# Eight more prompt tokens by gathered expert rows, and gathers released by TensorE's column blocks

## The reference

```python
def block(hb):
    q = rms_norm(jnp.einsum('td,dq->tq', hb, w_query).reshape(PEER_BLOCK, PEER_HEADS, PEER_DKEY), qnorm_g)
    s1 = jnp.einsum('thc,hnc->thn', q[..., :half], subkeys[:, 0])
    s2 = jnp.einsum('thc,hnc->thn', q[..., half:], subkeys[:, 1])
    v1, i1 = lax.top_k(s1, PEER_TOPK)
    v2, i2 = lax.top_k(s2, PEER_TOPK)
    ...
    sc, ci = lax.top_k(cand, PEER_TOPK)
    e = i1[ci // 16] * PEER_NKEYS + i2[ci % 16]
    g = jax.nn.softmax(sc, axis=-1)
    a = jax.nn.gelu(jnp.einsum('td,ted->te', hb, u[e]), approximate=False)
    return jnp.einsum('te,ted->td', g * a, v[e])
```

## Time and profile before

| | |
|---|---|
| Median of three runs | 1819.66 us |
| The profiled execution | 1820.75 us, span 1818.9 us |
| TensorE busy | 1766.4 us, 97% of the span |
| VectorE / ScalarE / GpSimd busy | 1214.8 / 565.8 / 487.9 us |
| DMA | 394.47 MB, 217 GB/s over the span |
| The costliest line | L2111, matmuls of the v stage |

### The profile page before, as it was taken

One profiled execution on the slowest core, in us unless ns is written; L12 is line 12 of the kernel. 1 busy time (PEld: TensorE's weight loads), 2 busy tenths in 40 slices (PEclk: granted clock), 3 DMA queues, 4 the chain that ended last, 5 costly groups with the idle time before them and its releaser, 6 DMA issues.

```text
span 1818.9 us, 30885 instructions
## 1 busy us (share of the span) xinstructions
PE 1766.4 (97%) x12693; PEld 1305.6 (72%) x12693; DVE 1214.8 (67%) x2531; ACT 565.8 (31%) x944; POOL 487.9 (27%) x531
## 2 busy tenths in 40 slices
PE   8999898999999999999999999999979999999999
PEld 7744446788888888898888888888636666666665
DVE  7559777768989948787365555544336666666664
ACT  1003234502233233545254444443212222222220
POOL 0000201011656710000000000000457676776750
PEclk9999999999999999999999999999979999999999
DMA  4423723012113334666988888775678888888881
GB/s 168 114 85 122 241 94 140 1 73 93 47 70 141 140 141 164 255 255 244 325 293 295 294 298 293 263 262 175 249 272 331 334 335 335 342 334 335 337 335 48
DMA packets 135885, 394.47 MB, mean 217 GB/s; under 512 B 12992, under 2 KB 85936, under 8 KB 123968
## 3 DMA queue, kind: packets, MB, share of 16 engines
q1 hardware_dynamic: 109392, 315.29, 46.9%
q0 software_dynamic: 26352, 77.20, 12.1%
HBM read 316.52 MB, written 75.92 MB: 216 GB/s over the span
## 4 chain that ended last, share of the span: by engine, by line
PE 81%; DVE 13%; DMA 2%; issue 2%; SPq 1%; ACT 1%; DVEq 0%; ACTq 0%
PE psum L2063 32%; PE psum L2111 28%; PE psum L1764 16%; PE psum L2084 2%; DVE u_lo L1517 1%; DMA qrow<-d_q 1%; DMA u_raw<-in_uT 1%; PE psum L1893 1%; DVE kprod L1182 0%; DVE sSc L1183 0%; DVE rest L1444 0%; DVE sdm L1321 0%; PE psum L1916 0%; PE psum L1816 0%; DMA xT<-in_xT 0%
## 5 line engine op out<-in xcount | busy, mean ns | idle before, releaser
L2111 PE MATMUL psum<-w_hl,v_hi 128*128 128x384 bf16 x2048 | 504.2, 328 | 7.9 <-issue 7.9
L2063 PE MATMUL psum<-h_hi,u_hi 128*128 128x260 bf16 x2048 | 394.0, 273 | 4.7 <-DVE u_lo L1517 3.8
L2063 PE MATMUL psum<-h_lo,u_hi 128*128 128x260 bf16 x2048 | 393.8, 273 | 0.0
L2063 PE MATMUL psum<-h_hi,u_lo 128*128 128x260 bf16 x2048 | 393.7, 273 | 0.0
L753 POOL DMA_INDIRECT trow<-in_v,t_lists x136 | 170.7, 1255 | 696.1 <-ACT act_f L971 589.9
L2111 PE MATMUL psum<-w_hl,v_lo 128*128 128x384 bf16 x1024 | 335.8, 328 | 7.0 <-issue 7.0
L2111 PEld LDWEIGHTS psum<-w_hl,v_hi 128*128 128x128 bf16 x2048 | 200.8, 98 | 147.8 <-issue 18.3
L1674 DVE TENSOR_TENSOR v_lo<-v_raw,v_hi 128x1024 bf16<-128x1024 f32 x128 | 148.2, 1219 | 166.0 <-ACT v_hi L988 102.4
L988 ACT ACTIVATE v_hi<-v_raw 128x1024 bf16<-128x1024 f32 x128 | 124.7, 1044 | 373.8 <-PE psum L2111 361.2
L1517 DVE TENSOR_TENSOR u_lo<-u_raw,u_hi 128x1024 bf16<-128x1024 f32 x128 | 154.0, 1217 | 118.1 <-ACT u_hi L959 118.0
L2063 PEld LDWEIGHTS psum<-h_hi,u_hi 128*128 128x128 bf16 x2048 | 196.7, 97 | 35.7 <-DVE u_lo L1517 4.3
(11 more groups left out here) (382 smaller groups left out, 1784.0 us busy)
## 6 DMA issues: line engine op xcount, KB each, us to landing
u_raw<-in_uT SPq DMA_DIRECT2D x32, 2048.0 KB, 9.3
v_raw<-in_v SPq DMA_DIRECT2D x32, 2048.0 KB
wr<-in_w SPq DMA_DIRECT2D x13, 2048.0 KB, 7.5
d_gate<-stage SPq DMA_DIRECT2D x12, 2048.0 KB, 7.2
w_hl<-d_w SPq DMA_DIRECT2D x32, 768.0 KB
g_up<-d_gate SPq DMA_DIRECT2D x18, 768.0 KB, 9.2
d_w<-w_up SPq DMA_DIRECT2D x18, 768.0 KB, 10.3
d_act<-act_f SPq DMA_DIRECT2D x14, 768.0 KB, 4.1
```

The source lines that it names most:

```text
L2063: mm = pe.matmul(upair[n % 2][:, f, 0:HALF], w[g % 2][:, k, c * P:(c + 1) * P], hs[:, k, halves[f]], start=(k == 0 and x == 0), stop=(k == ...
L2111: mm = pe.matmul(ybank[m][:, 0:DENSE], w[g % 2][:, c, m * P:(m + 1) * P], w_hl[g % WRING][:, z, c, :], start=(g == 0 and c == 0 and x == 0 ...
```

## The change

Eight more prompt tokens (384 - 8 = 376 dense, `EXTRA` = 8) go by gathered rows. Their 8 x 128 experts fill eight more slots, 144 in all. They lie on the partitions as (half, head, token), so `x_acc` is folded by a small product with `xsel` in the last group. Twelve more list steps make their lists in `x_lists`, and GpSimd moves these to `t_lists` by 16 small DMAs. Stores and the gates keep 384 columns (`GATED`); only the last matmul operand is cut to 376. There is one pair of gate blocks fewer (47).

The order of the gathers changes too. `w_used` now counts column blocks, eight a group. GpSimd first waits for all stores and the last weighing, sends `LEAD` = 6 gathers of activations, and then one row and one gather of activations in turn, each row after `paced(s)` column blocks. The batch is four slots with four semaphores instead of eight with two. At the start x comes in four loads instead of eight.

```diff
+GATED = SEQ - P
+EXTRA = 8
+DENSE = GATED - EXTRA
+NBLK = GATED // TB
...
+XSLOTS = SSLOTS + EXTRA * H * TOPK // P
+TSLOTS = XSLOTS + H * TOPK
+BATCH = 4
+LEAD = 6
+DOTS = 4
+KEPT = EXTRA + P + DB
+HALVES = P // (EXTRA * H)
...
+def paced(s):
+
+    return max(0, KT * (NG - 2) * s // TSLOTS - 3)
...
-            for k in range(KT):
-                sp.dma_start(xT[:, k, :], I["xT"][:, k, :]).then_inc(x_in[k], 16)
-                if k == 1:
+            for k in range(0, KT, 2):
+                sp.dma_start(xT[:, k:k + 2, :], I["xT"][:, k:k + 2, :]).then_inc(x_in[k // 2], 16)
+                if k == 0:
...
                 if j >= WRING:
-                    sp.wait_ge(w_used, j - WRING + 1)
+                    sp.wait_ge(w_used, KT * (j - WRING + 1))
...
+            for half in range(HALVES):
+                for h in range(H):
+                    at = EXTRA * (H * half + h)
+                    pool.dma_start(t_lists[at:at + EXTRA, :, SSLOTS:XSLOTS],
+                                   x_lists[P - EXTRA:P, :, h * TOPK + half * (XSLOTS - SSLOTS):][:, :, 0:XSLOTS - SSLOTS]
+                                   ).then_inc(s_moved, 16)
...
-            pool.wait_ge(s_moved, 32)
+            pool.wait_ge(s_moved, MOVED)
             pool.wait_ge(a_gelu, NKEYS)
-            for s in range(4):
-                slot_row(s)
             for b in range(2):
                 pool.wait_ge(as_stored[b], 16 * (NG // 2))
                 pool.wait_ge(a_stored[b], 16 * (EARLY // 2))
-            for s in range(BATCH):
+            pool.wait_ge(w_prod, LATE_KEYS)
+            for s in range(LEAD):
                 slot_dot(s)
-            pool.wait_ge(w_prod, LATE_KEYS)
-            for s in range(4, TROWS):
+            for s in range(TSLOTS):
+                if paced(s) > 0:
+                    pool.wait_ge(w_used, paced(s))
                 slot_row(s)
-            for s in range(BATCH, 2 * BATCH):
-                slot_dot(s)
-            for s in range(TROWS, TSLOTS):
-                slot_row(s)
-                if s + 2 * BATCH - TROWS < TSLOTS:
-                    slot_dot(s + 2 * BATCH - TROWS)
+                if s + LEAD < TSLOTS:
+                    slot_dot(s + LEAD)
...
+            tail = slice(P - COLT, P)
+            first, second = idx[tail, NPT - 2, 0, :], idx[tail, NPT - 2, 1, :]
+            sdo(v.tensor_copy(x_gate[tail, :], gt[tail, NPT - 2, :]))
+            sdo(ts(t_who[tail, :], t_who[tail, :], -float(P), None, ALU.add))
+            sdo(ts(t_tmp[tail, 0, :], second, float(KEPT), t_who[tail, :], ALU.mult, ALU.add))
...
+            sdo(v.tensor_reduce(xsel[:, :], ident.rearrange("p (h t) -> p t h", t=EXTRA), AX.X, ALU.add))
...
+                if i == 1:
+                    v.wait_ge(s_moved, MOVED)
...
-                            mm = pe.matmul(ybank[m][:, 0:DENSE], w[g % 2][:, c, m * P:(m + 1) * P], w_hl[g % WRING][:, z, c, :],
+                            mm = pe.matmul(ybank[m][:, 0:DENSE], w[g % 2][:, c, m * P:(m + 1) * P], w_hl[g % WRING][:, z, c, 0:DENSE],
...
                     if g == NG - 1:
                         pe.wait_ge(t_added, TSLOTS)
-                        turn(ybank[m][:, DENSE:SEQ], t_acc[:, m * P:(m + 1) * P], P).then_inc(y_made, 1)
-                    elif m == (3 if g == 0 else KT - 1):
+                        product(ybank[m][:, DENSE:GATED], [(x_acc[:, m * P:(m + 1) * P], xsel[:, :])])
+                        turn(ybank[m][:, GATED:SEQ], t_acc[:, m * P:(m + 1) * P], P).then_inc(y_made, 1)
+                    else:
                         mm.then_inc(w_used, 1)
```

More of the change, by code:

```diff
@@ L200, in trunk_and_peer @@
     t_who = put("t_who", [P, 1], F32, c0 + 4928 + 20 * TSLOTS)
+    xsel = put("xsel", [P, EXTRA], F32, c0 + 8064)
     ones_row = put("ones_row", [H, SEQ], F32, c0)
@@ L356, in trunk_and_peer @@
     t_acc = put("t_acc", [P, D], F32, B0 + 12288)
+    x_acc = put("x_acc", [P, D], F32, B0)
+    x_lists = put("x_lists", [P, 3, P], F32, T0 + 40960)
+    x_vrow, x_arow, x_gate = x_lists[:, 0, :].bitcast(U32), x_lists[:, 1, :].bitcast(U32), x_lists[:, 2, :]
+    assert T0 + 40960 + 1536 <= W0
     upair = [pa[:, 2 * b:2 * b + 2, :] for b in range(2)]
@@ L378, in sems @@
         return [sem(n) for n in names.split()]
-    x_in = [sem(f"x_in{k}") for k in range(KT)]
+    x_in = [sem(f"x_in{k}") for k in range(KT // 2)]
     par_in, const_in, wg_in, cst_in = sems("par_in const_in wg_in cst_in")
@@ L417, in trunk_and_peer @@
     t_row_in = [sem(f"tile_row_in{b}") for b in range(TROWS)]
-    t_dots_in = [sem(f"tile_dots_in{b}") for b in range(2)]
+    t_dots_in = [sem(f"tile_dots_in{b}") for b in range(DOTS)]
     y_out = sem("y_out")
     SQUARES = KT - 1
+    MOVED = (2 + HALVES * H) * 16
     CONV_OUT, KP_OUT, VP_OUT, MS_OUT, CP_OUT, SML_IN = 3 * 16, (NPT + 1) * 16, (NPT + 1) * 16, 3 * 16, 2 * 16, 9 * 16
@@ L552, in store_gates @@
             def store_gates(n):
-                sp.wait_ge(gl_ev, (n + 1) * QUADS)
+                sp.wait_ge(gl_ev, min((n + 1) * QUADS, NQUADS))
                 sp.dma_start(d_gate[n], stage[n % 2][:, :, :]).then_inc(g_stored[n % 2], 16)
@@ L594, in _ @@
                 for pair in gate_pairs_at(n):
-                    if pair % (QUADS // 2) == QUADS // 2 - 1:
+                    if pair % (QUADS // 2) == QUADS // 2 - 1 or pair == NPAIRS - 1:
                         store_gates(pair // (QUADS // 2))
@@ L784, in _ @@
             for k in range(KT):
-                act.wait_ge(x_in[k], 16)
+                act.wait_ge(x_in[k // 2], 16)
                 A(hT[:, k, :], xT[:, k, :], ACT.Copy, scale=par[:, P_G1 + k:P_G1 + k + 1]).then_inc(h_done, 1)
@@ L985, in v_high @@
                 if g >= 2:
-                    act.wait_ge(w_used, g - 1)
+                    act.wait_ge(w_used, KT * (g - 1))
                 for s in range(GC):
@@ L1078, in _ @@
             for k in range(KT):
-                v.wait_ge(x_in[k], 16)
+                v.wait_ge(x_in[k // 2], 16)
                 do(tt(sqT[:, k, :], xT[:, k, :], xT[:, k, :], ALU.mult), sq_done)
@@ L1632, in _ @@
             sdo(stt(t_tmp[:, 0, :], t_tmp[:, 0, :], float(P * GC), t_tmp[:, 1, :], ALU.mult, ALU.add))
-            sdo(stt(t_vrow[:, SSLOTS:TSLOTS], second, float(GC), t_tmp[:, 0, :], ALU.mult, ALU.add))
+            sdo(stt(t_vrow[:, XSLOTS:TSLOTS], second, float(GC), t_tmp[:, 0, :], ALU.mult, ALU.add))
+            tail = slice(P - COLT, P)
[3 more added lines that the diff above has]
+            sdo(ts(t_tmp[tail, 0, :], second, float(KEPT), t_who[tail, :], ALU.mult, ALU.add))
+            sdo(stt(x_arow[tail, :], first, float(KEPT * P), t_tmp[tail, 0, :], ALU.mult, ALU.add))
+            sdo(v.tensor_copy(t_int[tail, 0, :], first))
+            sdo(ts(t_int[tail, 1, :], t_int[tail, 0, :], 2, None, ALU.logical_shift_right))
+            sdo(v.tensor_copy(t_tmp[tail, 0, :], t_int[tail, 1, :]))
+            sdo(ts(t_int[tail, 1, :], t_int[tail, 0, :], 3, None, ALU.bitwise_and))
+            sdo(v.tensor_copy(t_tmp[tail, 1, :], t_int[tail, 1, :]))
+            sdo(stt(t_tmp[tail, 0, :], t_tmp[tail, 0, :], float(P * GC), t_tmp[tail, 1, :], ALU.mult, ALU.add))
+            sdo(stt(x_vrow[tail, :], second, float(GC), t_tmp[tail, 0, :], ALU.mult, ALU.add))
+            sdo(v.tensor_reduce(xsel[:, :], ident.rearrange("p (h t) -> p t h", t=EXTRA), AX.X, ALU.add))
             first, second = idx[0:n64, NPT, 0, 0:TOPK], idx[0:n64, NPT, 1, 0:TOPK]
@@ L1636, in _ @@
             sdo(v.tensor_tensor_reduce(s_junk[:, :], seld, iota[0:n64, 0:DB], 1.0, 0.0, ALU.mult, ALU.add, s_who[:, :]))
[L1637 removed]
+            sdo(ts(s_who[:, :], s_who[:, :], float(EXTRA + P), None, ALU.add))
             sdo(ts(s_tmp[:, 0, :], second, float(KEPT), s_who[:, :], ALU.mult, ALU.add))
@@ L1672, in v_low @@
                 if g >= 2 and s == 0:
-                    v.wait_ge(w_used, g - 1)
+                    v.wait_ge(w_used, KT * (g - 1))
                 tt(v_lo[g % 2][:, s, :], v_raw[g % 2][:, s, :], v_hi[g % 2][:, s, :], ALU.subtract).then_inc(vlo_done, 1)
@@ L1705, in slot_row @@
                     b = s // BATCH
-                    v.wait_ge(t_dots_in[b % 2], 16 * BATCH * (b // 2 + 1))
+                    v.wait_ge(t_dots_in[b % DOTS], 16 * BATCH * (b // DOTS + 1))
                     if s == 0:
-                        v.wait_ge(s_moved, 32)
+                        v.wait_ge(s_moved, MOVED)
                     sdo(tt(t_wts[:, s:s + BATCH], t_dots[:, s:s + BATCH], t_gate[:, s:s + BATCH], ALU.mult), t_weighed)
                 v.wait_ge(t_row_in[s % TROWS], 16 * (s // TROWS + 1))
-                acc = s_acc if s < SSLOTS else t_acc
-                if s in (0, SSLOTS):
+                acc = s_acc if s < SSLOTS else x_acc if s < XSLOTS else t_acc
+                if s in (0, SSLOTS, XSLOTS):
                     ins = ts(acc[:, :], trow[s % TROWS][:, :], t_wts[:, s:s + 1], None, ALU.mult)
```

41 lines of the change are left out of this document (18 added, 23 removed).

## The result

The changed kernel takes 1808.53 us (median of four runs, 1806.37 to 1810.27) against 1820.49 of the kernel before in the same job. The ratio is 0.9931, 95% interval 0.9915 to 0.9947, so it is faster by 0.7%. The forecast was 1809.5. The profiled execution took 1809.43 us, 11.3 less than the profiled one before.

What follows compares the result with a forecast made beforehand. TensorE, busy 97% of the span, was taken as the bound. The terms -10.2 - 0.9 + 3.2 + 1.7 - 1.0 - 3 = -10.2 us took the median from 1819.66 to 1809.5; the 8-in-10 range was 1785 to 1826.

Steps and rivals of the forecast that it cites:

- Columns, -10.2: In the v stage, matmuls over 376 instead of 384 columns were to save 10.2 us, 15.28 us a group instead of 15.60.
- Pair of gate blocks, -0.9: One pair of gate blocks fewer on TensorE (48 to 47) was to save 0.9 us.
- List steps, +3.2: VectorE's twelve more list steps ahead of the first gate rows, for which TensorE waits, were to cost 3.2 us.
- my bound of 4.9: Upper bound for the list steps: 4.9 us if the longer gap also drops the clock for some us (1.7 lost).
- Products, +1.7: Eight products of x_acc by xsel on TensorE in the last group were to cost 1.7 us.
- Start, -1.0: At the start, four loads of x instead of eight were to shorten TensorE's wait for the squares by 1.0 us.
- More slots, 0: Eight more gathered slots were to cost 0, covered on VectorE, Pool and DMA, with the DMA share at 0.92.
- The hole, -3: TensorE's "issue" gaps and slow clock early in the v stage, 24.2 us, were to cost 3 us less through pacing.
- full DMA engines for over 20 us: Nearest to a cause of the v stage's 24.2 us hole: a full DMA stretch over some 20 us; called a correlation.
- the sum of the backlog: From 1291, queues of 10.50 and 7.35 MB keep DMA full past 1311, so the hole should open again.
- the hole that is gone: Rival: spread-out gathers break the full DMA stretch before 20 us, TensorE never starves; 1788.3 us, chance 0.26.
- the hole as before: Rival: the v stage's hole goes by something other than the backlog and stays; 1812.5 us, chance 0.19.

Runs made afterwards that it cites:

- columns_384: The changed kernel with the last matmuls over all 384 columns again; 1817.29 us.
- changed_again: The changed kernel itself, measured once more in the second job; 1808.13 us.
- lists_early: The changed kernel with all of VectorE's list steps moved ahead of its copies of the transposed tables; 1799.59 us, ratio 0.9910.
- lists_136: The kernel before with the new order of gathers alone (136 slots, 384 columns) and its list steps moved ahead of the tables; 1799.34 us.
- pacing_alone: The kernel before with only the new order of gathers and the four loads of x (136 slots, 384 columns); 1804.26 us, ratio 0.9914.
- lists_early_again: The changed kernel with the list steps ahead of the tables, measured a second time; 1800.46 us, ratio 0.9900.
- no_rows: The changed kernel with the gathers of v rows left out but for the first ten slots; 1805.45 us.
- lists_late1: The changed kernel with list steps ahead of the tables and gathers starting one group later, spread over 29 groups; 1791.09 us, ratio 0.9859.
- late_no_rows: The changed kernel with gathers two groups later and v rows left out but for the first ten slots; 1793.34 us.

## Why the prediction was right, and where its steps were off

The time, the sign and the range held. The terms did so only in part, and two misses offset each other: the v stage was to start 1.3 us later (-0.9 + 3.2 - 1.0) and started 5.8 later, and the hole was to cost 3 us less and cost 8.1 less. That the sum came within 1 us of the median is luck.

- **Columns, -10.2.** Right: 15.28 us a group in the trace, 9.2 us between `columns_384` and `changed_again`.
- **Pair of gate blocks, -0.9.** Nothing in the runs isolates it. With the list steps hidden in both, the v stage starts at 1288.2 with 47 pairs and at 1289.7 with 48 (`lists_early`, `lists_136`), which is in keeping with it.
- **List steps, +3.2.** Right in place, too small. The wait for the gate rows grew by 3.1 us (1.0 to 4.1), just the sum. But the longer gap dropped the clock, which my bound of 4.9 allowed for and my value left out, and the drop was twice as long as I took. In the changed kernel the clock was at 0.57 in the 8 us from 712 to 720, about 3.4 us lost. Moving the steps brought the start of the v stage 7.3 us forward, the old 1.0 of wait included; with 136 slots, where only the old steps move, it came 2.1 us forward (1291.87 to 1289.74), so the twelve new ones cost about 5. The medians fell by 7.7 to 8.9 us, by the ratios to the kernel before 4 to 6.
- **Products, +1.7.** Too large: in the last group product and transpose take 0.12 + 0.16 us a column block instead of 0.11 for the transpose alone, so 8 x 0.17 = +1.4. (The matmuls of a block went from 1.95 to 1.91, but that belongs to the columns.) I had taken the price of eight such products in a row, 0.21 each; alone between long matmuls one takes 0.12. Why isn't shown.
- **Start, -1.0.** Not there: the wait for the squares is 6.0 us in one piece instead of 5.6 in two. Between the start and the gate rows the changed kernel lost 1.3 us in stretches at 1.2 GHz in the first 320 us, and `pacing_alone`, which has the same loads, starts its v stage 2.2 us late. None of this is shown to come from the loads.
- **More slots, 0.** Right for the waits: VectorE, GpSimd and the v tiles hold nothing up in the steady part, and the share is 0.93. Probably too low if the holes are counted, since `pacing_alone` without these slots had 1.3 us of hole and the median of `lists_136` equals that of `lists_early_again`, though its matmuls are longer.
- **The hole, -3.** The direction was right and the size was off: 24.2 to 16.1 in this profile, 14.3 in another. Two steps behind the term failed. The first is that `paced` shortens the hole by holding rows from 11 on back. The first row held was row 12, for 2.74 us, and it went out at 1344.69, 0.4 us after the hole had ended; and it was held because the signal came late, since its 17 blocks were done near 1336.4. The second is that full DMA engines for over 20 us open the hole. Two kernels had 39 and 49 us of that without one, and in `no_rows` it went on with the engines empty. So the sum of the backlog had the right sign by a rule that doesn't hold. What went with the smaller hole is that the rows started 18 us later (1309.11 instead of 1291.19); no run takes that alone.
- **Chances.** "The two likeliest lie together, from 1804 to 1815" doesn't fit the list above it: the second likeliest case there is the hole that is gone (0.26, at 1788.3), ahead of the hole as before (0.19). The range and the sums by threshold use the list and stand.

The rule of the Trainium skill that I set against this term ("SBUF — State Buffer", section "Who interferes with whom": DMA never contends with a compute engine) isn't contradicted by these traces: `lists_late1` and `pacing_alone` ran TensorE at full pace beside full DMA engines. But what I drew from it, that pacing the gathers leaves the hole as it is, was wrong: `pacing_alone` took 14 us off the time, with a hole of 1.3 us in its profile instead of 24.2.

**What stays open.** What TensorE waits for in the hole. Its matmuls come there in groups of one to five that start about 0.7 us apart or a multiple of it (1312.58, 1313.29 and 1314.00 in the kernel before), the profile names no releaser, and its length differs between two profiles of the same program (16.1 and 14.3). It is nearly absent in the profiles of `late_no_rows`, `lists_late1` and `pacing_alone`, and no order of release sets these three apart: `lists_136` releases by the same counts as `pacing_alone` and had 8.3 us of it. The 24 runs of the kernel before in the first job spread from 1800.58 to 1823.83, so even the old order probably runs almost without it at times, but no such run was profiled. A late instruction block, semaphore signals of TensorE that get through late (as seen by ScalarE and GpSimd), a limit on SyncE's or GpSimd's side and a limit of TensorE itself are all left; no run here tells them apart. Why `lists_late1` is better than `lists_early` is open too.

## What to carry to other kernels

Price a step by its place in the engine's order: twelve instructions of 0.3 us on an engine that is idle a third of the time cost about 5 us, since TensorE was waiting on that chain and the gap dropped its clock; moved 10 us earlier into an idle stretch they cost nothing that the profile shows. When a change has two parts, run each part alone: here the new order of the gathers by itself gave as much as the whole change, and the 10 us that the extra tokens' shorter matmuls save went back into stalls and the list wait. Where times of one kernel fall into groups, compare a profile's own time with the median before a number from it is taken as typical. And before a limit is credited with a gain, see in the trace whether it ever held anything back: the counts of `paced` hardly did where the hole was. A correlation seen once in one profile, like full DMA engines beside the hole, deserves a run that has the one without the other before it is put in a sum.

## What I had not expected of the hardware

A stall of TensorE with no releaser on record, worth 16 to 24 us in the two profiles of before and after and 8 to 15 us in nine of the twelve other profiles, one piece or several, while in three it is nearly absent (0.1 to 1.8 us). Beside full DMA engines for 49 us (share 1.02) TensorE was busy 48.73 of 49 us (`lists_late1`). In the hole of the changed kernel, finished column blocks became known to ScalarE and GpSimd 12 and 8 us late. And waits aren't free: 128 instructions that only wait for a semaphore already there went with a wait of 15.0 us at the start, where it had been 6.0 anyway, so about 9 us came on top, and the v stage began 9.9 us later.
